# Decoder-layer kernel: query and key transposes on the DMA crossbar from step 4 on, a separate query norm chain from step 5 on, and a reordered head

## What is computed

```python
ada = jax.nn.silu(c) @ w_ada + b_ada                     # adaLN vector
shift, scale, gate = jnp.split(ada, 3, axis=-1)
h = rms_norm(x, norm_g) * (1.0 + scale[:, None, :]) + shift[:, None, :]
z = h @ w_in
for g, (window, dilation) in enumerate(ATTN_GROUPS):     # 3 groups, 8 heads of 64 each
    q = partial_rope(rms_norm(qkv[:, :, g, 0], q_norm_g[g]), positions)
    k = partial_rope(rms_norm(qkv[:, :, g, 1], k_norm_g[g]), positions)
    v = qkv[:, :, g, 2]
    o, lse = dilated_window_attention(q, k, v, window, dilation)
# softmax mixture of the three groups, times a SiLU gate: branch A
# chunked gMLP: branch B; gated merge, output projection, residual
```

## Time and profile before

| | us |
|---|---|
| median of 3 runs (lowest, highest) | 726.0 (724.86, 728.2) |
| the profiled execution: its own time | 726.06 |
| the profiled execution: span of its slowest core (core 3) | 724.4 |
| spans of the 8 cores, lowest and highest | 720.3 to 724.4 |
| TensorE busy in the span of core 3 | 703.7 (97%) |
| VectorE, ScalarE, GpSimd busy | 448.8, 362.6, 295.5 |

### The profile page before, as it was taken

One profiled execution on the slowest core, in us unless ns is written; L12 is line 12 of the kernel. 1 busy time (PEld: TensorE's weight loads), 2 busy tenths in 40 slices (PEclk: granted clock), 3 DMA queues, 4 the chain that ended last, 5 costly groups with the idle time before them and its releaser, 6 DMA issues.

```text
span 724.4 us, 14426 instructions; the slowest of 8 cores (720.3 to 724.4 us)
## 1 busy us (share of the span) xinstructions
PE 703.7 (97%) x4651; PEld 352.4 (49%) x4651; DVE 448.8 (62%) x778; ACT 362.6 (50%) x704; POOL 295.5 (41%) x386
## 2 busy tenths in 40 slices
PE   7789999999999999999999999999999999999997
PEld 2344455446666665555554444444444444444443
DVE  5447799875687788887777864565844232232234
ACT  2646888887655455567776545664221111111110
POOL 1715244353455565533334004567233343433435
PEclk9879999999999999999999999999999999999999
DMA  8997135782556667651424258049970223211234
GB/s 236 306 195 170 59 84 124 109 99 57 73 79 100 86 89 89 88 102 26 94 30 81 53 116 146 1 77 177 187 235 24 88 88 83 91 59 58 63 113 174
DMA packets 73817, 76.27 MB, mean 105 GB/s; under 512 B 49168, under 2 KB 55696, under 8 KB 73488
## 3 DMA queue, kind: packets, MB, share of 16 engines
q1 hardware_dynamic: 52768, 41.67, 25.2%
q0 software_dynamic: 18528, 25.43, 23.7%
q10 hardware_dynamic: 2448, 8.26, 2.8%
HBM read 74.82 MB, written 8.39 MB: 115 GB/s over the span
## 4 chain that ended last, share of the span: by engine, by line
PE 83%; DMA 4%; ACT 3%; DVE 3%; SPq 3%; issue 2%; POOL 2%; ACTq 0%; DVEq 0%; POOLq 0%
PE ps L237 72%; DMA arena<-x 3%; PE ps L662 3%; ACT arena L246 3%; DVE arena L246 3%; PE ps L698 3%; POOL arena L246 2%; PE ps L702 2%; PE ps L540 2%; SPq L249 1%; PE ps L355 1%; SPq L725 1%; PE ps L210 1%; SPq L604 0%; PE ps L1098 0%
## 5 line engine op out<-in xcount | busy, mean ns | idle before, releaser
L237 PE MATMUL ps<-arena 128*128 128x512 bf16 x2604 | 577.4, 379 | 0.5 <-DVE arena L246 0.4
L237 PEld LDWEIGHTS ps<-arena 128*128 128x128 bf16 x2604 | 272.2, 107 | 276.2 <-issue 7.7
L246 POOL TENSOR_TENSOR arena<-arena 128x128 bf16<-128x128 f32 (+5 forms) x308 | 253.1, 830 | 356.8 <-DVE arena L246 282.6
L246 ACT ACTIVATE arena<-ps 128x1024 bf16<-128x1024 f32 (+3 forms) x292 | 197.0, 706 | 238.8 <-PE ps L237 144.2
L246 DVE TENSOR_TENSOR arena<-ps,arena 128x512 bf16<-128x512 f32 (+3 forms) x215 | 155.1, 726 | 71.5 <-ACT arena L246 32.8
L246 ACT ACTIVATE arena<-arena 128x8 f32<-128x8 f32 (+7 forms) x286 | 118.7, 423 | 84.3 <-DVE arena L246 55.8
L246 DVE SCALAR_TENSOR_TENSOR arena<-arena,ps 128x512 f32<-128x512 f32 x80 | 54.4, 686 | 106.9 <-PE ps L237 86.3
L246 DVE TENSOR_TENSOR arena<-arena 128x1024 bf16<-128x1024 bf16 (+5 forms) x112 | 77.1, 691 | 20.7 <-POOL arena L246 10.7
L246 DVE TENSOR_REDUCE arena<-arena 128x8 f32<-128x512 bf16 x96 | 65.1, 681 | 27.5 <-ACT arena L246 27.3
L229 POOL DMA_DIRECT2D arena<-w_in x42 | 24.5, 604 | 49.9 <-PE ps L237 30.2
L246 DVE SCALAR_TENSOR_TENSOR arena<-arena 128x512 f32<-128x512 f32 (+3 forms) x40 | 32.6, 816 | 13.8 <-DMA arena<-w_adag 6.2
(11 more groups left out here) (44 smaller groups left out, 167.4 us busy)
## 6 DMA issues: line engine op xcount, KB each, us to landing
arena<-x SPq DMA_DIRECT2D x30, 512.0 KB, 5.0
arena<-w_in POOLq DMA_DIRECT2D x44, 256.0 KB, 4.7
out<-arena ACTq DMA_DIRECT2D x15, 512.0 KB, 5.2
arena<-w_ada SPq DMA_DIRECT2D x12, 512.0 KB, 12.9
arena<-w_in POOLq DMA_DIRECT2D x6, 1024.0 KB, 10.4
arena<-arena SPq DMA_DIRECT2D x32, 128.0 KB, 2.4
arena<-w_adag SPq DMA_DIRECT2D x8, 512.0 KB, 8.3
arena<-w_out POOLq DMA_DIRECT2D x2, 1024.0 KB, 23.4
```

What stands on the lines that cost most here:

```text
L237: ins = e.matmul(out_ap, l, r, start=(i == 0), stop=(i == n - 1))
L246: P.op(eng, lambda e: getattr(e, meth)(*a, **kw), reads=reads, writes=writes)
```

## The change

Four things change.

1. `transp` and `kgain` use the DMA transposes from step 4 instead of step 8, and the loop issues them at the start of the iteration accordingly.
2. `QS` goes from 9 to 5, so iterations 5 to 8 get the separate chain for q.
3. In the head, the third adaLN column is finished after two of the eight additions of the fourth block instead of four; `x_mods` and the spins are reordered (three spins ahead of the transposes of x tile 3, sixteen behind it instead of nineteen); the first piece of q is projected for steps 0 to 2 ahead of the fourth column. The rest of steps 0 to 3 is rewritten: v's pieces, the q projection of step 4 and the v projection of step 3 stand ahead of the k transposes; `x_moda` gives half of tile 4 to ScalarE; x tile 5 is prepared in one place of the head.
4. Iteration 4 is written out in an order of its own: the k and v projections earlier, x tile 6 prepared in it, k of step 2 and v of step 3 copied out of PSUM by VectorE. The one key `hd`, on which all early writes of the k and v buffers stood, becomes one key for each buffer.

```diff
...
         ada_mm(2)
+        spin(3, 7)
         sq_own(3)
         x_prep(3)
         x_transp(3, 6)
-        ada_sum(3, 0, 4)
+        spin(4, 7)
+        ada_sum(3, 0, 2)
         ada_ab(2)
+        for kc in (0, 1):
+            x_mods(kc, "act", 2, 2)
         for kc in (4, 5):
             x_mods(kc, "act", 0, 2)
-        for kc in range(6):
+        for kc in range(2, 6):
             x_mods(kc, "act", 2, 2)
         for j in (0, 1, 2):
             for p_ in range(4):
...
             x_load(t + 4, gate=[("ws2p1", "ws2p3")[t - 2]])
-        ada_sum(3, 4, 8)
-        spin(7, 7, ["wada3_0"])
-        spin(7, 7, ["wada3_2"])
-        spin(5, 7, ["wada3_4"])
-        ada_col(3)
-        for kc in (6, 7):
-            x_mods(kc, "act", 0, 2)
-            x_mods(kc, "dve", 2, 2)
+        ada_sum(3, 2, 8)
+        for k_ in ("hm2_0", "hm2_1", "hm0_4"):
+            spin(4, 7, [k_])
         g2_ = gqk.rearrange("p (g r) -> p g r", r=2)
...
         def kgain(s):
-            if 8 <= s < 47:
+            if 4 <= s < 47:
...
             q_ = qi(s)
-            if 8 <= s < 47:
+            if 4 <= s < 47:
...
 
-        def last(role):
-            for s in range(4):
+        def x_moda(t, bank):
+            for kc in range(4, 8):
+                X("act", "activation", [B(bank), "hm%d_3" % t, "ab%d" % (kc // 2)], ["hm%d_%d" % (t, kc)], out=hT[:, kc, 128 * t:128 * (t + 1)],
+                  in_=psb[:, bank, kc, :], func=AF.Identity, scale=ab[:, 8 + kc:9 + kc], bias=ab[:, kc:kc + 1])
+
+        def half(role, s):
+            rstd2(s, role)
+            for u in (s, s + 1):
+                scaleqk(u, role)
+            rope2(s, role)
+
+        def last(role, ss):
+            for s in ss:
                 proj_part(s, role, 3)
                 sumsq(s, role)
-                if s == 2:
-                    rstd2(0, role)
-                    for u in (0, 1):
-                        scaleqk(u, role)
-                    rope2(0, role)
-                    if role == 0:
-                        sq_own(4)
-                        rs_own(4)
-                        sc_own(4)
-                if s == 3 and role == 1:
-                    phase(2, 0, (0, 1))
-                    proj(4, 0)
-                    transp(2, (0,), 2)
-                    sq_own(5)
-                    rs_own(5)
-            rstd2(2, role)
-            for u in (2, 3):
-                scaleqk(u, role)
-            rope2(2, role)
+        phase(0, 0, range(3))
+        ada_col(3)
+        for kc in (6, 7):
+            x_mods(kc, "act", 0, 2)
+            x_mods(kc, "dve", 2, 2)
+        phase(0, 1, range(3))
+        phase(0, 0, (3,))
+        phase(0, 1, (3,))
+        phase(0, 2)
+        last(0, range(2))
+        half(0, 0)
+        last(0, range(2, 4))
+        sq_own(4)
+        rs_own(4)
+        sc_own(4)
+        half(0, 2)
         for j in range(3):
-            phase(0, j)
-        last(0)
-        phase(1, 0)
-        phase(1, 1)
+            phase(1, j)
+        x_transp(4, TH)
+        last(1, range(2))
+        transp(0, (0,), 0)
+        transp(1, (0,), 1)
+        x_mod(4, TH, 0, 4)
+        half(1, 0)
+        last(1, range(2, 4))
         x_load(8)
-        phase(1, 2)
-        x_transp(4, TH)
-        x_mod(4, TH)
-        for s in range(2):
-            transp(s, (0,), s)
-        last(1)
-        sumsq(4, 0)
-        phase(2, 1, (0, 1))
-        phase(2, 0, (2,))
-        phase(2, 1, (2,))
+        x_moda(4, TH)
+        half(1, 2)
+        sq_own(5)
+        rs_own(5)
         sc_own(5)
         x_load(9)
+        phase(2, 0, range(3))
+        phase(2, 1, range(3))
         phase(2, 2, range(3))
-        transp(0, (1,), 3)
-        transp(1, (1,), 4)
+        proj(4, 0)
+        sumsq(4, 0)
+        transp(2, (0,), 3)
         rstd(4, 0, 8)
         for s in range(3):
             proj_part(s, 2, 3)
-            vevac(s, "act" if s == 1 else "dve")
+        vevac(0, "dve")
+        transp(0, (1,), 3)
+        transp(1, (1,), 4)
         scaleqk(4, 0)
-        x_transp(5, TB)
-        x_mod(5, TB)
+        vevac(1, "dve")
+        vevac(2, "dve")
+        for j in range(4):
+            proj_part(3, 2, j)
+        x_transp(5, 0)
+        x_mod(5, 0)
         scores(0, 0)
         mask(0, 0)
-        transp(2, (1,), 0)
-        for j in range(4):
-            proj_part(3, 2, j)
-        vevac(3)
-
-        QS = 9
+
+        QS = 5
...
         for tb in range(2):
             for hp in range(4):
@@ -879,7 +888,7 @@
         fin_at[47] = (0, 2)
         for it in range(4, NS):
             a, b_, c_ = it - 1, it - 3, it - 4
-            if 8 <= a < 16:
+            if 4 <= a < 16:
                 transp(a)
             if it > 4:
                 proj(it, 0)
@@ -887,10 +896,21 @@
             if it - 1 in fin_at:
                 finZ(*fin_at[it - 1])
                 finA(*fin_at[it - 1])
+            if it == 4:
+                proj(it, 1)
             if not one(b_):
                 scores(b_, 0)
             if it == 4:
+                transp(2, (1,), 0, "dve")
+                square(it, 1)
                 x_sq(6, ssqk[qi(4)][:, 16:17], "ssq%d2" % qi(4))
+                vevac(3, "dve")
+                proj(it, 2)
+                sumsq(it, 1, False)
+                rstd(4, 8, 17)
+                x_scale(6, rsqk[qi(4)][:, 16:17], "rs%d2" % qi(4))
+            if it == 5:
+                x_sq(7, ssqk[qi(5)][:, 16:17], "ssq%d2" % qi(5))
             if it >= QS:
                 rstd(it, 0, 8)
             if it >= 16 and not one(b_):
@@ -900,19 +920,26 @@
             if 5 < it + 1 < NT:
                 x_transp(it + 1, TB)
                 x_mod(it + 1, TB)
-            proj(it, 1)
-            square(it, 1)
+            if it > 4:
+                proj(it, 1)
+                square(it, 1)
             if it >= QS:
                 scaleqk(it, 0)
-            sumsq(it, 1, False)
+            if it > 4:
+                sumsq(it, 1, False)
             if it < 16 and not one(b_):
                 mask(b_, 0)
             scores(b_, 1)
+            if it == 4:
+                transp(3)
+                vevac(it)
             pv(c_)
             if it < 18:
                 kgain(it - 2)
-            if it < 16:
-                rstd(it, 0 if 4 < it < QS else 8, 17 if it + 2 < NT else 16)
+            if it == 4:
+                pass
+            elif it < 16:
+                rstd(it, 0 if 4 < it < QS else 8, 17 if 4 < it < NT - 2 else 16)
                 if 4 < it < QS:
                     scaleqk(it, 0)
             else:
@@ -923,7 +950,8 @@
                 finB(*fin_at[it - 1])
             scaleqk(it, 1)
             if it + 2 < NT:
-                x_scale(it + 2, rsqk[qi(it)][:, 16:17], "rs%d2" % qi(it))
+                if it > 4:
+                    x_scale(it + 2, rsqk[qi(it)][:, 16:17], "rs%d2" % qi(it))
                 if it + 6 < NT:
                     x_load(it + 6)
             for n in (0, 1):
@@ -936,13 +964,14 @@
             if it < 16:
                 accum(c_, 1)
             accum(c_, 0)
-            proj(it, 2)
-            vevac(it)
-            if not 8 <= a < 16:
+            if it > 4:
+                proj(it, 2)
+                vevac(it)
+            if a >= 16:
                 transp(a)
             if it in (39, 43, 47):
                 spread((it - 39) // 4)
-            if it + 3 < NT:
+            if 4 < it < NT - 3:
                 x_sq(it + 3, ssqk[qi(it + 1)][:, 16:17], "ssq%d2" % qi(it + 1))
             if 6 <= it < 10:
                 load_w(3, 3072, it - 6, it - 5)
...
```

More of the change, by code:

```diff
@@ L290, in build_nc @@
               compare_op=op_, fill=0.0, base=0, channel_multiplier=cm_)
+        HD = ["hk%d" % i for i in range(NK)] + ["hv%d" % i for i in range(NV)]
         so = A.at(off_ring + 1024 * NQ, [128, 3584], F32)
@@ L304, in build_nc @@
         flo = frq[:, 8:16].unsqueeze(1).to_broadcast([128, 48, 8])
-        X("dve", "tensor_copy", ["misc", "hd"], ["posf"], out=posf, in_=posi)
+        X("dve", "tensor_copy", ["misc"] + HD, ["posf"], out=posf, in_=posi)
         X("dve", "tensor_tensor", ["posf", "misc"], ["kf"], out=kf, in0=bc(posf, 8), in1=flo, op=ALU.mult)
@@ L319, in build_nc @@
             if nm == "sinT":
-                X("act", "activation", ["yy", "hd"], [nm], out=tab, in_=yy, func=AF.Sin)
+                X("act", "activation", ["yy"] + HD, [nm], out=tab, in_=yy, func=AF.Sin)
         def rot_tables(g, q="pool"):
@@ L326, in rot_tables @@
                 for T_, tab, nm in ((T1, cosT, "cosT"), (T2, sinT, "sinT")):
-                    X(q, "tensor_tensor", [nm, "misc", "hd"], ["T%d_%d" % (1 if T_ is T1 else 2, g)],
+                    X(q, "tensor_tensor", [nm, "misc"] + HD, ["T%d_%d" % (1 if T_ is T1 else 2, g)],
                       out=T_[:, gi, :, :].rearrange("p b (u d) -> p b u d", u=2),
@@ L436, in x_mods @@
                   op0=ALU.mult, op1=ALU.add)
-        sq_own(0)
         def x_prep(t):
@@ L617, in transp @@
```

(4 more changed lines are left out.)

## The result

The median of the changed kernel is 722.01 us (720.18 to 722.41), beside 725.85 us for the kernel before in the same comparison. The ratio of the runs is 0.9938, with a 95% interval of 0.9908 to 0.9967. The forecast was 721.8 us, faster, in a range of 719.5 to 725.0. The total is right. Its parts are not: the head won 1.9 us more than the sum had on core 5, and what lies behind step 5 lost 2.6 us that the sum did not have.

A forecast was written before the change was run, and what follows sets the result against it. TensorE, busy 97% of the span, was taken as the bound. Core 5, slowest after the change: 723.2 - 2.6 + 0.3 - 2.0 - 0.25 + 1.0 + 0.5 = 720.15, plus 1.66 around the span: 721.8 us, range 719.5 to 725.0.

The forecast's parts named there:

- -2.6 and +0.3: Iterations 5 to 8: 2.6 us won by taking on iteration 9's period, 0.3 us lost as VectorE's shown lag.
- 4 x 0.45 = 1.8: Iterations 5 to 8: eight q and k transposes taken off TensorE in each, 0.45 us apiece, 1.8 of the 2.6 us.
- 1.7 us of cover: Loop: x's next tile is written out by 118.59, the projection needing it begins at about 120.3, hiding VectorE's lag.
- the first rival: VectorE or ScalarE becomes the bound of iterations 4 to 8; price 1.9 us, so 723.7 us; chance 0.20.
- The four waits: Head: TensorE's waits ahead of q or k transposes and tile 5's, all closed: 2.35 us on core 3, 2.0 on core 5.
- ScalarE's in iteration 4, +1.0: Iteration 4: tile 6's transposes wait for ScalarE to empty bank 3; 1.0 us, between bounds 0 and 2.0.
- The weights' wait, +0.5: Head: third v piece asked for as its weights land; 0.5 us on core 5, none on core 3, bounds 0 and 1.6.
- the 1.6: Front, core 3: third k piece starts at 55.8 instead of 57.4 us if the clock comes up; 1.6 us, lower bound 0.
- the sum's 3.2: Added DMA transposes: slack between first issue and k's gain (9.4 us) and the longest landing (6.2 us).
- The slower rival: DMA transposes land later than k's gain needs, in ScalarE's queue in iterations 6 to 9; 730 us; chance 0.05.

The follow-up runs named there:

- run with the copies moved: Changed kernel with the copies of the denominators moved from VectorE to ScalarE for steps 1 to 4 too: 720.67 us, ratio 0.9943 to the kernel before.
- second execution: Changed kernel run once more, unchanged, on the chip of the last four runs: 720.92 us, ratio 0.9946 to the kernel before.
- run with the later gain: Changed kernel with the gain of k behind pv from iteration 18 on too, about 3 us later: 719.59 us, ratio 0.9933 to the kernel before.

## Why the prediction was right, and where not

**The loop: right sum, wrong division.** Forecast -2.6 and +0.3, measured -2.51 on core 5 and -2.3 on the cores whose first iteration takes 7.53. Pricing the new iteration by the one that already works that way, 7.39, held. The step "4 x 0.45 = 1.8 is work taken off TensorE, the rest is waits and breaks in the stream" fails as a reason: with that work off and nothing else changed, the four iterations take 0.8 more. A period that a ring of waits sets is not shortened by what TensorE saves in it.

**VectorE's lag: mis-sized cover, and later than thought.** The sum counted 0.3 as shown, and the rest hidden by 1.7 us of cover. In the changed kernel VectorE runs at 7.43 in iterations 5 to 8 with a single wait of 0.27 in each (timeline, core 5), and TensorE's transposes of an x tile start 0.15 behind the end of VectorE's scaling of that tile (98.70 + 0.74 = 99.44):

```profile
98.09 0.69 DVE L246 TENSOR_TENSOR arena<-ps,arena 128x512 bf16<-128x512 f32 x1 [0.27 <-ACT arena L246]
98.70 0.74 DVE L246 TENSOR_SCALAR arena<-arena 128x1024 bf16<-128x1024 f32 x1
99.36 1.16 DVE L246 TENSOR_TENSOR arena<-arena 128x1024 bf16<-128x1024 bf16 x1
...
105.52 0.69 DVE L246 TENSOR_TENSOR arena<-ps,arena 128x512 bf16<-128x512 f32 x1 [0.27 <-ACT arena L246]
...
143.16 0.69 DVE L246 TENSOR_TENSOR arena<-ps,arena 128x512 bf16<-128x512 f32 x1 [0.62 <-ACT arena L246]
```

```profile
99.59 0.61 PE L356 MATMUL ps<-arena 128*128 128x128 bf16 x8
```

The cover that I named belongs to another operation of the same queue, the write-out of the tile behind its transposes. The link that binds is the scaling ahead of them, and it has next to none. So the first rival, VectorE as the bound, was right in kind: the pace of steps 1 to 10 is VectorE's and ScalarE's, 7.43 to 7.47 instead of 7.39, and one iteration takes 7.81, where TensorE waits 0.36 for that scaling. It was wrong in price: 0.6 us in steps 5 to 10, not 1.9 in 1 to 5 (its 723.7 also counts 0.3 of that twice). Steps 5 to 10 take 36.98 to 37.09 us in the three kernels where q shares k's chain up to step 8, so the 0.6 comes with q's own chain. That moving the copies only moves it shows that the copies are not at fault. In the long iteration VectorE waits 0.62 for ScalarE at 143.16 instead of 0.27, and 0.63 in the long iteration of the run with the copies moved; why just there, I did not settle.

**The head: two terms too dear.** The four waits closed as said. Of the new waits set against them, ScalarE's in iteration 4, +1.0, did not come: on core 5 the trace lists no wait of TensorE from 56.5 to 80 us, and on the other cores none for ScalarE. I took the middle between two bounds; the lower one was right. The weights' wait, +0.5 on core 5, was 0 there. On cores 1 and 3 it was 0.87 and 0.92, at the third v piece (core 4 has 0.97 at the same place, put down to VectorE), within the bound of 1.6 but on cores that came early. Together with the 0.48 that core 5 won ahead of tile 4, by a weight transfer that landed sooner in that execution (executions differ by more than this), these make 1.9 us.

**The front: right at 0, no sign of the 1.6.** On core 5 it won nothing by itself, as said. The 1.6 were for a core whose clock is late, and on the few such cores (above) the new front shows no lead. The late start is about as frequent with either front, on too few cores to tell more. Core 3's gain of 6.3 us at step 1 (85.42 to 79.14) is thus in large part the absence of a late start: 4.6 of it come ahead of x tile 4's transposes (59.16 to 54.52), where the other cores gain 0.0 to 1.5.

**The DMA transposes: hidden in steps 4 to 7, as said.** On core 5 the first pair is issued at 80.06 and its gain of k runs at 88.61, so 8.55 us behind it, and the landings there are 2.5 to 6.4 us. The slack was less than the sum's 3.2, which counts from the first of a pair: k's is the second, issued 1.3 us later here, so 7.2 us are left for it. The slower rival has its mechanism elsewhere: not ScalarE's queue in iterations 6 to 9, but VectorE's from iteration 18 on. It was there before the change, and I did not look.

**What would have shown it wrong:** `pv` marks 7.4 to 7.5 apart, right, but for the 7.53 of some first iterations; no wait on the k transposes, right; the third k piece behind a wait for `w_in` on most cores, wrong, only on cores 0 and 1 (0.29 and 0.24). Of the signs against it, a clock at 1.2 GHz through the first projections came on core 2 of the second execution.

So the total was right because two errors of opposite sign met: 2.1 us too little gain up to step 5, and 2.6 us of loss behind it. That is luck: 0.6 of the loss is the ring's, and the other 2.0 are for the larger part not the change's, as far as the executions show. The second series comes out at 3.9 us below the kernel before, near the forecast too, but with another core as the slowest, in the profiled execution one with a late start.

## What to carry to other kernels

Before pricing a saving on the busiest engine, ask whether its period is its own work or a ring of waits through the others; in a ring, two edits can each be worth nothing and, as here, 2.5 us together, so try them in pairs. For cover, take the operation of a queue that the waiting engine needs first, not the one with the most room. Where an engine stops in order for a transfer, asking for it later costs nothing if nobody needs the result sooner.

## What the runs showed of the hardware

Two things that I had not expected. The mask of the second half of the scores on VectorE takes 1.16 us at 99.36 above, and that of the first half 0.68, 2.2 us earlier, where GpSimd does not rotate beside it (the changed kernel, VectorE, then GpSimd, core 5):

```profile
97.14 0.68 DVE L246 TENSOR_TENSOR arena<-arena 128x1024 bf16<-128x1024 bf16 x1
```

```profile
98.94 3.29 POOL L246 TENSOR_TENSOR arena<-arena 128x256 f32<-128x256 bf16 x4 [3.56 <-DVE arena L246]
```

The rotation is longer too, 3.29 us beside 2.49 where the two do not meet. That is so in iterations 10 to 13 of the same kernel, where GpSimd issues a weight load ahead of the rotation (GpSimd, then VectorE, whose mask there is the line at 121.68):

```profile
122.85 2.49 POOL L246 TENSOR_TENSOR arena<-arena 128x256 f32<-128x256 bf16 x4
```

```profile
115.65 0.69 DVE L246 TENSOR_REDUCE arena<-arena 128x8 f32<-128x512 bf16 x1 [0.27 <-ACT arena L246]
...
121.68 0.68 DVE L246 TENSOR_TENSOR arena<-arena 128x1024 bf16<-128x1024 bf16 x1
...
123.11 0.69 DVE L246 TENSOR_REDUCE arena<-arena 128x8 f32<-128x512 bf16 x1 [0.75 <-ACT arena L246]
```

The Trainium skill, "SBUF — State Buffer", section "SBUF: two separate sides", says that a VectorE operation with two SBUF inputs and a GpSimd operation that reads SBUF exclude one another on a shared port for a whole instruction; the rows agree, with 0.48 us a mask. What that is worth in the ring, iterations 10 to 13 show: nothing there. The mask is 0.48 shorter, VectorE waits 0.48 longer for ScalarE behind it (0.75 instead of 0.27, in iterations 10 to 12), and the `pv` marks are still 7.46 or 7.47 apart.

And TensorE's clock: a wait of 1.94 us for a weight piece, just as the projections began, was followed by seven microseconds at 1.2 GHz on core 2 of the second execution, which put step 1 some 3 us later there and made it the slowest of the eight. On core 4 of that execution a wait of 2.71 at the same place was followed by 0.50 until 44 us. Waits of 0.4 to 0.9 there on cores 0, 1, 3 and 4 in the first execution of the changed kernel left the clock at 1.00. The length of the wait alone does not decide it: one of 1.69 on core 2 of the first execution and one of 1.79 on core 7 of the run with the copies moved left it at 1.00. Nor does every late start come from such a wait: on cores 0 and 7 of the run with the later gain the clock was at 0.50 from 38 us on, through the spins, ahead of the wait.
